# Two layers of a hybrid encoder on one core: another router, an earlier ranking of the experts, and another order of the first expert loads

## What is computed

```python
h = rms_norm(x, norm2_g) * (1.0 + scale2) + shift2       # 256 x 1024
logits = h @ router_w                                    # 256 x 8
top_val, top_idx = lax.top_k(logits, 2)
gates = softmax(top_val)
# each token goes to its two experts; an expert is
y_e = (silu(h_e @ w1[e]) * (h_e @ w3[e])) @ w2[e]        # 1024 -> 3584 -> 1024
x = x + gate2 * sum_of_the_two(gates * y_e)
```

## Time and profile before

| | |
|---|---|
| three runs | median 1339.88 us (1339.25 to 1344.27) |
| the profiled execution | 1338.82 us |
| its span | 1337.1 us |
| PE busy | 1288.1 us, 96% |
| PEld busy | 951.8 us, 71% |
| DVE busy | 912.9 us, 68% |
| ACT busy | 734.2 us, 55% |
| read by DMA | 474.91 MB |

### The profile page before, as it was taken

How to read it: one execution, slowest core, us unless ns; L and a number is a source line. 1 busy time by engine, 2 the same in 40 slices (tenths; PEclk the granted TensorE clock), 3 DMA queues, 4 the chain that set the end, 5 groups by cost and what they waited for, 6 DMA issues and landing times.

```text
span 1337.1 us, 20638 instructions
## 1 busy us (share of the span) xinstructions
PE 1288.1 (96%) x7976; PEld 951.8 (71%) x7976; DVE 912.9 (68%) x1523; ACT 734.2 (55%) x1267; POOL 4.0 (0%) x37
## 2 busy tenths in 40 slices
PE   7999999999999999999999999998998999989996
PEld 5875899999988996566857888855865754257531
DVE  4788898888787558676869998835966653066411
ACT  4655654444455457566839998735945653055310
POOL 0000000000000000000000000000000000000000
PEclk9999999999999999999999999998999999899999
DMA  9995768879758377999999999999999999999997
GB/s 343 372 329 198 270 228 299 302 292 334 278 196 293 127 272 258 391 417 405 421 417 412 412 409 414 414 405 416 408 422 412 417 421 419 422 405 420 420 420 299
DMA packets 130145, 474.91 MB, mean 355 GB/s; under 512 B 9437, under 2 KB 11626, under 8 KB 107514
## 3 DMA queue, kind: packets, MB, share of 16 engines
q1 hardware_dynamic: 128672, 472.28, 89.9%
q10 hardware_dynamic: 1370, 1.25, 0.3%
HBM read 472.46 MB, written 1.05 MB: 354 GB/s over the span
## 4 chain that ended last, share of the span: by engine, by line
PE 77%; DMA 9%; DVE 7%; SPq 4%; ACT 2%; issue 1%; DVEq 0%; ACTq 0%
PE bank L1845 10%; PE bank L1848 10%; PE bank L1846 10%; DMA ring<-in_moe_w 6%; PE bank L1969 6%; SPq L903 4%; PE bank L1364 3%; PE bank L1361 3%; PE bank L1360 3%; DMA beside_out<-in_moe_w 2%; PE bank L1757 2%; PE bank L1670 2%; PE bank L1404 2%; PE bank L1402 2%; PE bank L1108 2%; PE bank L1409 2%
## 5 line engine op out<-in xcount | busy, mean ns | idle before, releaser
L2459 ACT ACTIVATE hi_first<-ring 128x512 fp32r<-128x512 f32 x156 | 95.8, 631 | 54.6 <-DMA ring<-in_moe_w 34.9
L3338 DVE TENSOR_TENSOR lo_first<-ring,hi_first 128x512 fp32r<-128x512 f32 x156 | 102.0, 687 | 30.8 <-ACT hi_first L2459 30.5
L3338 DVE TENSOR_TENSOR lo_third<-ring,hi_third 128x512 fp32r<-128x512 f32 x150 | 98.0, 687 | 34.0 <-ACT hi_third L2459 33.3
L3338 DVE TENSOR_TENSOR lo_second<-ring,hi_second 128x512 fp32r<-128x512 f32 x154 | 100.6, 687 | 29.3 <-ACT hi_second L2459 28.6
L2459 ACT ACTIVATE hi_second<-ring 128x512 fp32r<-128x512 f32 x154 | 95.4, 631 | 39.5 <-PE bank L1848 34.2
L2459 ACT ACTIVATE hi_third<-ring 128x512 fp32r<-128x512 f32 x150 | 92.5, 632 | 30.3 <-DMA ring<-in_moe_w 14.3
L2752 DVE SCALAR_TENSOR_TENSOR ada_acc<-ring,c_act,ada_acc 128x512 f32<-128x512 f32 x140 | 105.1, 751 | 3.9
L1969 PE MATMUL bank<-ring,work 128*32 128x512 f32 x686 | 91.2, 597 | 6.8 <-DMA ring<-in_moe_w 4.8
L2082 ACT ACTIVATE w_hi<-ring 128x1024 fp32r<-128x1024 f32 x66 | 68.8, 1054 | 47.5 <-PE bank L1409 23.6
L2987 DVE TENSOR_TENSOR w_lo<-ring,w_hi 128x1024 fp32r<-128x1024 f32 x66 | 79.4, 1221 | 10.3 <-ACT w_hi L2082 10.2
L1360 PE MATMUL bank<-hg_hi,w_hi 128*128 128x256 f32 x336 | 82.7, 284 | 0.0
(11 more groups left out here) (578 smaller groups left out, 3195.8 us busy)
## 6 DMA issues: line engine op xcount, KB each, us to landing
ring<-in_moe_w SPq DMA_DIRECT2D x207, 1024.0 KB, 18.9
ring<-in_ada_w SPq DMA_DIRECT2D x24, 2048.0 KB, 12.2
ring<-in_moe_w SPq DMA_DIRECT2D x45, 768.0 KB, 14.2
ring<-in_ffn_w SPq DMA_DIRECT2D x15, 2048.0 KB, 9.5
beside_out<-in_moe_w SPq DMA_DIRECT2D x17, 1024.0 KB, 18.3
beside_h<-in_moe_w SPq DMA_DIRECT2D x16, 1024.0 KB, 18.6
beside_x<-in_moe_w SPq DMA_DIRECT2D x15, 1024.0 KB, 21.6
beside_w<-in_moe_w SPq DMA_DIRECT2D x15, 1024.0 KB, 18.2
```

Of the source, the lines that this page charges most:

```text
L2459: A(hi_piece(Q), raw_piece(SPLITS[r], q, j), ACT.Copy).then_inc(hi_done, 1)
L3338: v.tensor_tensor(lo_piece(Q), raw_piece(SPLITS[r], q, j), hi_piece(Q).bitcast(F32), ALU.subtract).then_inc(lo_done, 1)
```

## The change

**Router on scaled tiles.** `normalise` writes scaled tiles without shift; the logits are taken from these, 16 products of 8 columns with the tokens on the output's partitions (L1622 of the changed kernel). What the shift adds to a logit is the same for all tokens: VectorE multiplies the router by the shift (`router_shift`), a product with ones sums it over the partitions (L1605), VectorE sums over k (`logit_shift`) and adds it at the logits. ScalarE writes h into `xT`, not in place. The quadrants, `fold` and the copy of the logits go. VectorE adds the squares of tiles 1 to 5 into tile 0, so TensorE sums three tiles, not eight, all behind the last piece. The second half of x's token rows is kept behind h's. Four `keep_pace` products go. `H_ORDER` is the order of h's transposes; `gains`, and the first low part (`split_to` of piece 0), stand earlier on VectorE.

**Ranking in front of the first gather.** `places()` follows `comparisons()` directly, ahead of `gathered(0)`. The loads into "lo" and "h" wait for the later readers of these places.

**Order of the loads.** `WOVEN` begins with slots 0 and 1 of expert 0, then all four w1 slots (eight halves) of the first light expert, then slots 2 to 4; from the sixth slot on it is as before. No load is put ahead as number 20; `s_places` is waited for behind load 19. The positions of the light expert's steps move from q = 4, 6, 9, 10 to 1, 2, 5, 6.

The core of the diff:

```diff
-WOVEN = ((0, 0, 3), (1, 0, 2), (0, 3, 4), (1, 2, 4), (0, 4, 5), (1, 4, 5), (0, 5, 6), (1, 5, 8), (0, 6, 9), (1, 8, 10), (0, 9, 10), (1, 10, 12),
+WOVEN = ((0, 0, 2), (1, 0, 4), (0, 2, 5), (1, 4, 5), (0, 5, 6), (1, 5, 8), (0, 6, 9), (1, 8, 10), (0, 9, 10), (1, 10, 12),
          (0, 10, 11), (1, 12, 14), (0, 11, 12), (1, 14, 16), (0, 12, 21), (1, 16, 23))
 WIDE_WOVEN = ((0, 8), (0, 4), (8, 10), (4, 9), (10, 11), (9, 14), (11, CUT), (14, None), (CUT, None))
 WOVEN_SILU = {0: {24: 0}, 5: {37: 0, 45: 1}}
...
-    PLACES_AT = 1
     GATES_AT = 8
     GAIN_AT = 57
-    TOKENS_AT = 4
+    TOKENS_AT = 1
     MEMBERS_AT = 14
-    MID_DISPATCH_AT = {0: 6, 3: 12, 5: 6}
+    MID_DISPATCH_AT = {0: 2, 3: 12, 5: 6}
     DISPATCH_AT = {"A": g_last["w3", 1] + 29, "C": XPT_AT + 3}
-    MID_GATHER_AT = {0: 9, 3: 21, 5: 18}
-    TURN_FIRST_AT = 10
+    MID_GATHER_AT = {0: 5, 3: 21, 5: 18}
+    TURN_FIRST_AT = 6
     GATHER_AT = g_last["w3", ECH - 1] + 5
     LOW_AT = GATHER_AT + 1
     LATE_DISPATCH_AT = 50
...
-    ahead += [(0, len(FIRST) // 2, len(FIRST) % 2)]
...
@@ -961,10 +959,10 @@
                 elif what == "hidden":
                     sp.wait_ge(g_free, GQ)
                 elif what == "lo":
+                    sp.wait_ge(s_lg, 2)
+                    sp.wait_ge(s_h, 4 * KT)
+                elif what == "h":
                     sp.wait_ge(s_ht, 4)
-                elif what == "h":
-                    sp.wait_ge(s_xt2, 4)
-                    sp.wait_ge(s_hp, 4 * KT)
                 else:
...
@@ -1591,9 +1589,7 @@
             by_pieces(6, (0, 1, 2), range(6, KT))
             by_pieces(6, (3,))
             by_pieces(7, (0, 1))
-            norm_sums(3, range(0, 2))
             by_pieces(7, (2, 3))
-            norm_sums(3, range(2, KT))
 
...
+            pe.wait_ge(s_evac, 30)
+            pe.wait_ge(s_pre, 1)
+            mm(psum[1][:, P:P + KT * NE].rearrange("p (k e) -> p k e", k=KT), ones[:], router_shift, start=True,
+               stop=True).then_inc(s_lg, 1)
+            pe.wait_ge(s_pre, 2)
+            mm(psum[6][:, 0:S], ones[:], rstd[:, 0, :], start=True, stop=False)
+            for k in (6, 7):
+                pe.wait_ge(s_sq, 24 + k + 1)
+                last = mm(psum[6][:, 0:S], ones[:], rstd[:, k, :], start=False, stop=(k == KT - 1))
+            last.then_inc(s_ssq, 1)
             pe.wait_ge(s_x, 32)
-            for n in range(4):
-                if n == 3:
-                    pe.wait_ge(s_xa, 1)
+            for n in range(3):
                 tokens_first(n, xT, X_BANKS[n], s_xt2)
-            keep_pace(2, 0)
-            pe.wait_ge(s_router, 16)
+            pe.wait_ge(s_root, ROOT["norm3"] + 1)
+            tokens_first(3, xT, X_BANKS[3], s_xt2)
+            pe.wait_ge(s_evac, 32)
             for k in range(KT):
-                j = k % 4
-                pe.wait_ge(s_h, 24 + k + 1)
-                last = mm(psum[6][32 * j:32 * (j + 1), 0:S], router[:, k, :], hT[:, k, :], start=(k < 4), stop=(k >= 4))
-            last.then_inc(s_lgr, 1)
-            pe.wait_ge(s_evac, 32)
-            tokens_first(0, hT, H_BANKS[0], s_ht)
-            pe.wait_ge(s_lge, 1)
-            pe.wait_ge(s_xa, 4)
-            for tt in range(TT):
-                last = mm(psum[7][:, S + tt * NE:S + (tt + 1) * NE], logits[:, tt * P:(tt + 1) * P], fold[:],
-                          start=True, stop=True)
+                pe.wait_ge(s_hp, 24 + k + 1)
+                for tt in range(TT):
+                    last = mm(psum[1][:, HALF + tt * NE:HALF + (tt + 1) * NE], hT[:, k, tt * P:(tt + 1) * P], router[:, k, 0:NE],
+                              start=(k == 0 and tt == 0), stop=(k == KT - 1), skip_group_check=True)
             last.then_inc(s_lg, 1)
-            for n in (1, 2, 3):
-                tokens_first(n, hT, H_BANKS[n], s_ht)
-
-            keep_pace(1, 0)
+            pe.wait_ge(s_xa, 2)
+            for n in H_ORDER:
+                pe.wait_ge(s_h, 24 + 4 * (n % 2) + 4)
+                tokens_first(n, xT, H_BANKS[n], s_ht)
+
...
-                        A(hT[:, k, :], hT[:, k, :], ACT.Identity, bias=mod[:, l, c + k:c + k + 1]).then_inc(s_h, 1)
+                        A(xT[:, k, :], hT[:, k, :], ACT.Identity, bias=mod[:, l, c + k:c + k + 1]).then_inc(s_h, 1)
 
             def evac(f, dst, func=ACT.Copy):
                 wait_filled(act, f)
...
-            for n in range(4):
+
+            def keep_x(n):
+
                 act.wait_ge(s_xt2, n + 1)
                 tt, half = divmod(n, 2)
                 A(x_acc[:, tt, half * 512:(half + 1) * 512], psum[X_BANKS[n]][:, :], ACT.Copy).then_inc(s_xa, 1)
+
+            keep_x(0)
+            keep_x(1)
+            act.wait_ge(s_xt2, 4)
             shift(3)
-            act.wait_ge(s_lgr, 1)
-            A(logits, psum[6][:, 0:S], ACT.Copy).then_inc(s_lge, 1)
-            for n in range(4):
-                act.wait_ge(s_ht, n + 1)
+            for i, n in enumerate(H_ORDER):
+                act.wait_ge(s_ht, i + 1)
                 tt, half = divmod(n, 2)
                 A(h_rows[:, tt, half * 512:(half + 1) * 512], psum[H_BANKS[n]][:, :], ACT.Copy).then_inc(s_hth, 1)
+            keep_x(2)
...
@@ -3173,13 +3177,43 @@
             g_split(26)
             head_gate(3).then_inc(s_of, 1)
             low_head(3)
+
+            def split_to(Q_end, Q_last):
+
+                while tiles_done[0] <= min(Q_end, Q_last):
+                    Q = tiles_done[0]
+                    r, part_no = divmod(Q - FQ, PIECE_PARTS * EQ)
+                    q, j = divmod(part_no, PIECE_PARTS)
+                    dve.wait_ge(hi_done, Q + 1)
+                    v.tensor_tensor(lo_piece(Q), raw_piece(SPLITS[r], q, j), hi_piece(Q).bitcast(F32),
+                                    ALU.subtract).then_inc(lo_done, 1)
+                    tiles_done[0] += 1
+
+            def add_squares(k):
+
+                dve.wait_ge(s_sq, 24 + k + 1)
+                return v.tensor_tensor(rstd[:, 0, :], rstd[:, 0, :], rstd[:, k, :], ALU.add)
+
+            gains(3)
+            dve.wait_ge(s_router, 16)
+            v.tensor_tensor(router_shift, router[:, :, 0:NE],
+                            mod[:, 1, 24:24 + KT].rearrange("p (k o) -> p k o", o=1).to_broadcast([P, KT, NE]),
+                            ALU.mult).then_inc(s_pre, 1)
             g_split(28)
             residual(1, 28, range(0, 1))
             g_split(30)
             residual(1, 28, range(1, 2))
+            link(add_squares(1))
+            split_to(piece_no(0, 0), piece_no(0, 0))
             g_split(31)
-            residual(1, 28, range(2, 4))
-            gains(3)
+            residual(1, 28, range(2, 3))
+            link(add_squares(2))
+            link(add_squares(3))
+            link(add_squares(4))
+            add_squares(5).then_inc(s_pre, 1)
+            residual(1, 28, range(3, 4))
+            dve.wait_ge(s_lg, 1)
+            v.tensor_reduce(logit_shift, psum[1][:, P:P + KT * NE].rearrange("p (k e) -> p e k", k=KT), AX_X, ALU.add)
             invert_root(3)
...
             dve.wait_ge(s_tables, 1)
-            dve.wait_ge(s_lg, 1)
-            link(v.tensor_copy(lg, psum[7][:, S:S + TT * NE].rearrange("p (t e) -> p t e", t=TT)))
+            dve.wait_ge(s_lg, 2)
+            link(v.tensor_tensor(lg, psum[1][:, HALF:HALF + TT * NE].rearrange("p (t e) -> p t e", t=TT),
+                                 logit_shift.rearrange("p (t e) -> p t e", t=1).to_broadcast([P, TT, NE]), ALU.add))
 
             all_pairs = [P, TT, NE, NE]
             mine = rt[:, 5, :].rearrange("p (t e o) -> p t e o", t=TT, o=1).to_broadcast(all_pairs)
...
@@ -3564,8 +3586,8 @@
                     v.tensor_tensor(dst, dst, psum[2 + n][:, :], ALU.add).then_inc(s_scb, 1)
                 dve.wait_ge(s_scb, 4 * out_no(m) + 4)
 
-            split_to(piece_no(0, 0), piece_no(0, 0))
             comparisons()
+            places()
             gathered(0)
             hosted = None
```

25 lines of the change are left out of this document (7 added, 18 removed).

## The result

The changed kernel takes 1345.19 us (median of 20 runs, 1340.39 to 1349.45) against 1340.43 (median of 20, 1339.25 to 1344.27). The ratio is 1.0027, 95% interval 1.0020 to 1.0034: 3.6 us slower, 2.7 to 4.6. The forecast was 1.0 us slower. The forecast's range, 1336.5 to 1345.0, holds the ratio times the median of before (1344.05), and misses the median of the 20 runs by 0.2 us. The profiled execution took 1344.27, with a span of 1342.5 us; 5.4 us longer than the one of before.

What follows compares the result with a forecast made beforehand. TensorE was taken to bound the kernel from 550 to 896, memory after. The router's 3.7 us gain pays for longer load waits, slot 4 ends 1.0 us later: 1340.9 us forecast, range 1336.5 to 1345.

Steps and rivals of the forecast that it cites:

- Who bounds: TensorE bounds from 550 to 896, memory after; what TensorE is early or late by at slot 4 is gained or lost.
- The router stretch: 490 to 515: normalising from 499.2, gather at 507.8, first product of expert 0 at 511.4, 3.7 us earlier.
- from there to the gather nothing changes: From VectorE having the logits (503.7) to the gather (507.8): 4.1 us, as before.
- rival (b): Clock falls at the router (1.7 us) and again before slot 2 (2.3 us more): 1345 us; chance 0.20.
- clock below 1.00 before the gather: Deciding point of the slower rival: TensorE's clock drops below 1.00 before the gather at 507.8.
- The light block: Eight light halves after slot 1, waiting on loads through four ring homes: from 511.4, ending at 540.9.
- Slots 2 to 4: Three slots of expert 0 behind the light halves: 18.2 us, slot 4 ending at 559.1 against 558.06.
- Nothing is added: Memory near 560: load 35, issued 1.0 us later, still finds the queue busy, so no cost.
- Rival (c): Bytes set the end: memory idles about 6 us in place of 12.5, 6.5 us back, 1333.4 us; chance 0.07.
- The sum: Profiled execution 1338.82 plus 1.0 us is 1339.8; the runs' median 1.06 above that, 1340.9; chance 0.46.

Runs made afterwards that it cites:

- fewer_early: Kernel before with loads 60 to 63 cut to half their bytes, 2 MB or 5.0 us of memory time less: ratio 0.9984, 2.1 us faster.
- fewer_late: Kernel before with loads 200 to 203 cut to half their bytes, 2 MB or 5.0 us of memory time less: ratio 0.9955, 6.0 us faster.
- order_alone: Kernel before with the new order of first slots, no load ahead and the ranking before the gather, but the old router: ratio 1.0026.
- pace_router: Changed kernel with one unread product of 512 columns ahead of each of the eight pairs of narrow router products: ratio to before 1.0046.
- keep_place: Changed kernel with an unused tensor of 8 columns where `fold` stood, so later tensors keep their old addresses: ratio to before 1.0023.
- fold_last: Kernel before with `fold` allocated behind `tri`, so `beside_h` and `beside_out` stand 32 bytes lower, no instruction changed: ratio 1.0003.
- fold_moved: Kernel before with `fold` allocated behind the small tensors; `beside_out` 32 bytes lower, `beside_h` at its old address, no instruction changed: ratio 1.0004.
- pace_block: Changed kernel with 22 unread products of 512 columns in the waits of the light block: ratio to before 1.0118.
- router_alone: Changed kernel with the order of loads and first slots put back as before; new router and early ranking stay: ratio to before 0.9989, 1.5 us faster.

## Why the prediction came out as it did

**Who bounds, right in the main.** TensorE waits for no load between 543 and 900, its delay at slot 4 (1.8 us) is still 2.0 at the gather at 811.68, the queue dips again at 870, and fewer_early and fewer_late show a border near 900. That what TensorE is late by at slot 4 is what the kernel loses is not shown so exactly. By these two profiles the delay shrank before 900, because the clock fell behind the gather near 860 in before and not in the changed kernel. The same light block, in the changed kernel and then in before:

```profile
871.33 2.78 PE L1967 MATMUL bank<-ring,work 128*32 128x512 f32 x24
```

```profile
870.88 2.78 PE L1969 MATMUL bank<-ring,work 128*32 128x512 f32 x24
```

That leaves 0.45 us, and yet the lag of the memory at 900 is 1.6. And order_alone, with its late start taken off, is 5.0 us behind at slot 4 where the changed kernel is 1.6, but the runs give both the same time (1.0026 and 1.0027).

**The router stretch, right in its parts, 1.35 us short in the sum.** The first product of expert 0 came 2.4 us earlier, not 3.7. Normalising began at 499.63 and not 499.2. This is no term of the forecast: that execution was 0.4 us late already ahead of everything the change touches (ScalarE writes `o_heads` at 470.19 and not at 469.75). The larger part is the term "from there to the gather nothing changes": 4.1 us were put in, and from 504.20, when VectorE has the logits, to 509.17 it is 5.0. The transposes of h took 3.49 us at half clock, so TensorE began to count the tokens at 507.27, 0.7 after VectorE had the selection, and ScalarE's copies of h and x ended late as well; the gather started at 509.17 rather than 507.8. Against pace_router, where they take 1.95 and the stretch from the last narrow product to the gather 4.1, about 0.9 of the 1.35 are the clock. The forecast had this as the deciding point of rival (b), "clock below 1.00 before the gather", and gave that 0.20 against 0.46. By windows of 1 us it fell at 503.7, while the last narrow products ran.

**The light block, right.** From the first product of expert 0 to the end of the block 29.5 us were predicted and 29.65 measured. The waits on the ring came where they were put, and were followed by products at the low clock. Through them the memory was full, so the low clock cost only the last half and the first piece of slot 2: 0.9 and 1.1 us more than at full clock (its six products took 2.6 us, those from 523.31 on 1.5). The Trainium skill's rule on oscillation (TensorE: Matmul & The Clock Gate, Part 1: The HAM clock gate), which the prediction set against the change, agrees with the window from 535 to 544 here, behind a wait of 2.27 us, 1.06 of work and a wait of 1.41, and with order_alone; the five halves ahead of that ran at full clock. Slots 2 to 4 took 17.5 us (18.2 predicted): 559.88 against 559.1.

**"Nothing is added" near 560, wrong; what it cost stays open.** I looked at load 35 of the kernel before only. In the changed kernel the next load was issued at 555.1, and the memory idled 4.9 us. What it had saved at the router was gone. TensorE waits for none of these loads until 900; but the nearest case on record, the 5.0 us of memory time that fewer_early saves behind 610, was worth 2.1 us (0.7 to 3.6) in the runs, so that this had no effect is not shown. Rival (c), bytes set the end, rested on these bytes staying saved: its price was wrong too.

**The sum, right in sign and mechanism, too small: 1.0 against 3.6 (2.7 to 4.6).** 0.8 us more come from slot 4: 1.35 at the router, less what the slots behind took less. Some 1.1 us are worked out for the loads behind 900 at 412 and not 413 GB/s, a term that the prediction lacks: removing `fold` was costed at nothing. With them the account stands at 2.9 us, which lies in the interval, but it is no proof: keep_place, without that term, is not clearly faster (1.0023), and the 1.8 us at slot 4 are a difference of two executions of which one, that of before, had a fall of the clock, worth 1.6 us, which three of eight profiles with this order lacked. Where the kernel before runs without it, the change costs more than 1.8 at slot 4. The last product (1.6 us in the profile's 5.4), the idle memory at 551 and the late starts (four of seven profiles with the new router, two of seven with the old one) may each carry a part of the rest as well. These runs don't divide it up.

**Rival (b)** described the course best, both falls of the clock included, and its 1345 is next to the measured median. But its terms were 1.7 and 2.3 us for the two falls, where the traces show about 0.9 and, beyond the 1.6 that the forecast had already put in, 0.4. So that its number fits is luck.

## What to carry over

When two resources take turns as the bound, follow both through the program: the end of a stage on the engine, and the bytes moved by then; a gain in one is kept only up to the place where the other takes over. A block of work whose later loads need the places of its earlier loads waits for a whole trip of the memory; splitting it once, with other work between, took all of them away but one of 1.0 us. A fall of the clock that comes in one execution and not in the next moved TensorE by 1.6 us here, as much as the edits did: look for it in several profiles before the difference of two is put down to an edit. And check what an edit does to the addresses of everything allocated behind the tensor that it removes.

## What the runs showed of the hardware

With the tensors behind `rt`, a load place among them, 32 bytes lower (fold_last against fold_moved), 103.03 and not 103.33 MB moved in 250 us with the DMA engines full. A product of 512 float32 columns takes two passes and 0.94 us on TensorE. By windows of 1 us, TensorE's granted clock fell from 1.00 (2.4 GHz) to 0.50 (1.2 GHz) at 503.7, behind 3.4 us of products of 8 columns in which TensorE was busy throughout, and came back at 507.1; with a product of 512 columns ahead of each pair (pace_router) it stayed at 1.00. It fell there in all six profiles with the new router and no such products, for about 3 us in five and for 10 us in pace_block. In the light block it fell at 534.4, in the wait of 1.41 us that follows one of 2.27 and 1.06 us of work, and was back at 544.7. Behind a single wait of 2.6 to 2.9 us in the old order it fell in some executions and not in others (0.57 on average from 550 to 554 in before, 1.00 in router_alone). The first 30 us took about 2 us more in six of the twelve experiments' profiles than in the others, with the same instructions.
